# Tile 0's products with the first two value blocks between the late one-hot groups

## What is computed

```python
top_s, pos = lax.top_k(cand_s, PEER_TOPK)
experts = jnp.take_along_axis(cand_i, pos, axis=-1)
g = jax.nn.softmax(top_s, axis=-1)
a = jax.nn.gelu(jnp.einsum("td,thkd->thk", xc, u_tab[ec]))
out = jnp.einsum("thk,thkd->td", gc * a, v_tab[ec])
```

## Time and profile before

| | us |
|---|---|
| median of 3 runs | 2034.71 |
| lowest and highest | 2032.02, 2037.82 |
| span of the profiled execution | 2037.1 |
| TensorE busy | 1798.6 (88%) |
| VectorE busy | 1505.6 (74%) |
| ScalarE busy | 925.5 (45%) |
| GpSimd busy | 617.3 (30%) |

### The profile page before, as it was taken

One profiled execution on the slowest core, in us unless ns is written; L12 is line 12 of the kernel. 1 busy time (PEld: TensorE's weight loads), 2 busy tenths in 40 slices (PEclk: granted clock), 3 DMA queues, 4 the chain that ended last, 5 costly groups with the idle time before them and its releaser, 6 DMA issues.

```text
span 2037.1 us, 28687 instructions
## 1 busy us (share of the span) xinstructions
PE 1798.6 (88%) x11068; PEld 1601.8 (79%) x11068; DVE 1505.6 (74%) x1987; ACT 925.5 (45%) x1474; POOL 617.3 (30%) x549
## 2 busy tenths in 40 slices
PE   6999999999999999956875343699999999999997
PEld 5999999999999887756765243588888888888886
DVE  4464444444465548989889899977888889999997
ACT  5444444444443441123434899733344443433433
POOL 0000000001045003467777677112111114433430
PEclk9999999999999999978998556799999999999999
DMA  9565556556466869999999999498999999999994
GB/s 313 164 171 164 166 174 173 166 168 176 144 183 210 323 231 418 369 402 416 402 404 414 372 398 399 178 351 344 392 403 370 398 376 396 410 396 405 401 406 185
DMA packets 293543, 627.88 MB, mean 308 GB/s; under 512 B 10364, under 2 KB 223405, under 8 KB 234958
## 3 DMA queue, kind: packets, MB, share of 16 engines
q0 software_dynamic: 48400, 343.95, 42.0%
q1 hardware_dynamic: 244558, 282.20, 40.6%
q10 hardware_dynamic: 496, 0.58, 0.1%
HBM read 622.45 MB, written 8.44 MB: 310 GB/s over the span
## 4 chain that ended last, share of the span: by engine, by line
PE 71%; DVE 11%; issue 5%; ACT 4%; POOL 4%; DVEq 3%; DMA 2%; SPq 0%; POOLq 0%; ACTq 0%
PE ps L2019 35%; PE ps L1680 24%; DVE u_ring L1495 5%; PE ps L1861 4%; PE ps L1847 3%; DVEq L1445 3%; DMA u_ring<-in_peer_u,idx_all 2%; POOL u_ring L699 1%; POOL u_ring L708 1%; ACT ones L1132 1%; PE ps L1786 1%; PE ps L1767 1%; PE ps L1924 1%; PE ps L1984 1%; PE ps L1776 1%
## 5 line engine op out<-in xcount | busy, mean ns | idle before, releaser
L1254 DVE TENSOR_TENSOR w_lo<-raw,w_hi 128x2048 fp32r<-128x2048 f32 x112 | 259.1, 2313 | 322.7 <-ACT w_hi L781 322.7
L1680 PE MATMUL ps<-act_hi,w_hi 128*128 128x256 f32 x1536 | 442.2, 288 | 4.6 <-DVE act_lo L1378 2.9
L1680 PE MATMUL ps<-act_lo,w_hi 128*128 128x256 f32 x1536 | 435.8, 284 | 0.0
L1680 PE MATMUL ps<-act_hi,w_lo 128*128 128x256 f32 x1536 | 435.8, 284 | 0.0
L1189 ACT ACTIVATE v_hi<-v_raw 128x2048 fp32r<-128x2048 f32 x128 | 245.6, 1919 | 403.2 <-PE ps L2019 204.7
L2019 PE MATMUL ps<-v_hi,c_hi 128*128 128x512 f32 x1024 | 402.9, 393 | 1.2 <-DVE c_lo L1574 1.2
L2019 PE MATMUL ps<-v_hi,c_lo 128*128 128x512 f32 x1024 | 403.2, 394 | 0.0
L2019 PE MATMUL ps<-v_lo,c_hi 128*128 128x512 f32 x1024 | 402.1, 393 | 0.0
L1570 DVE TENSOR_TENSOR v_lo<-v_raw,v_hi 128x2048 fp32r<-128x2048 f32 x128 | 293.5, 2293 | 68.8 <-ACT v_hi L1189 68.3
L1495 DVE CUSTOM_DVE_ANT_0 u_ring<-u_ring,ps 128x2048 f32<-128x2048 f32 x144 | 326.3, 2277 | 19.9 <-DMA u_ring<-in_peer_u,idx_all 19.8
L781 ACT ACTIVATE w_hi<-raw 128x2048 fp32r<-128x2048 f32 x112 | 214.1, 1911 | 262.2 <-PE ps L1680 217.5
(11 more groups left out here) (246 smaller groups left out, 2267.6 us busy)
## 6 DMA issues: line engine op xcount, KB each, us to landing
v_raw<-in_peer_v SPq DMA_DIRECT2D x128, 1024.0 KB
raw<-in_w_in SPq DMA_DIRECT2D x80, 1024.0 KB
raw<-in_w_out SPq DMA_DIRECT2D x16, 1024.0 KB
wq<-in_peer_w_q SPq DMA_DIRECT2D x8, 2048.0 KB, 11.5
raw<-in_w_br_a SPq DMA_DIRECT2D x16, 512.0 KB
bias_by_query<-bias_by_distance POOLq DMA_DIRECT2D x1, 4096.0 KB, 20.6
bias_st<-bias_by_query POOLq DMA_DIRECT2D x16, 256.0 KB, 4.7
raw<-in_w_br_b SPq DMA_DIRECT2D x16, 256.0 KB
```

Source lines behind the costliest of these rows:

```text
L1254: nc.vector.tensor_tensor(w_lo[:, j % NHL], raw[:, j % NRAW], w_hi[:, j % NHL].bitcast(F32), ALU.subtract).then_inc(lo_done, 1)
L1680: last = nc.tensor.matmul(out_ap, w_parts[wp][:, slot, k], act_parts[ap][:, k], start=(k == k0 and m == 0), stop=(k == k1 - 1 and m == 2))
```

## The change

Tile 0's 24 products with value blocks 0 and 1 are put between the late groups: one behind each of the groups 2 to 12, then three, five and five. `TILE0_UPTO` gives how many are made before each group. The parts that they need are made earlier, by GpSimd: block 0's high part in two halves behind the gathers (10, 8) and (10, 10), its low part in four quarters behind (10, 13), (11, 1), (11, 3) and (11, 6); block 1's behind the last of GpSimd's own products of unit 11. ScalarE makes the high parts of tile 0's two matrices at (11, 11), GpSimd their low parts. Behind the groups, ScalarE and VectorE make tile 1's, and TensorE tile 1's 24 products of blocks 0 and 1. From block 2 on the loop is as it was. Loads and late operations take other places: block 1 is loaded once the last VectorE group is multiplied, block 2 after four late groups; the first row gather waits for late group 11, the second for block 0.

```diff
+TILE0_UPTO = [0, 0, 0] + list(range(1, 12)) + [14, 19, 24]
+FIRST_HIGH = [(10, 8), (10, 10)]
+FIRST_LOW = [(10, 13), (11, 1), (11, 3), (11, 6)]
...
-    b = n + n // 3 if n < 12 else n + 4 - max(n - LATE_OPS, 0) // 10
+    b = 1 if n == 0 else n + 2 + n // 4 if n < 12 else n + 4 - max(n - LATE_OPS, 0) // 10
...
         load_v(0)
-        sp.wait_ge(pk_pe, 2)
+        sp.wait_ge(dc_pe, DVE_GROUPS)
+        load_v(1)
+        sp.wait_ge(c_pe, ACT_GROUPS + 4)
         load_v(2)
-        sp.wait_ge(c_pe, ACT_GROUPS + 4)
-        load_v(1)
         sp.wait_ge(c_pe, ACT_GROUPS + LATE_GROUPS)
         load_v(3)
...
+        def first_high(b, dst, cols):
+            return nc.gpsimd.tensor_copy(dst[:, cols], v_raw[b][:, cols])
+        def first_low(b, hi, cols):
+            return nc.gpsimd.tensor_tensor(v_lo[b][:, cols], v_raw[b][:, cols], hi[:, cols].bitcast(F32), ALU.subtract)
...
             gather(u_ring[:, SLOT[n]], u_tab, u, k).then_inc(u_in[SLOT[n]], 16)
+            if (u, k) in FIRST_HIGH:
+                if k == FIRST_HIGH[0][1]:
+                    pool.wait_ge(v_in[0], 16)
+                    pool.wait_ge(sw_ok, NU - 1)
+                h = FIRST_HIGH.index((u, k))
+                first_high(0, v_hi0, slice(D // 2 * h, D // 2 * (h + 1))).then_inc(vh0_ok, 1)
+            if (u, k) in FIRST_LOW:
+                pool.wait_ge(vh0_ok, 2)
+                last = first_low(0, v_hi0, quarter(FIRST_LOW.index((u, k))))
...
+        pool.wait_ge(ch0_ok, 1)
+        for b in range(2):
+            nc.gpsimd.tensor_tensor(c_lo[b][:, 0], ct[:, 0, b], c_hi[0][:, b].bitcast(F32), ALU.subtract).then_inc(first_ok, 1)
+        pool.wait_ge(v_in[1], 16)
+        pool.wait_ge(dc_pe, DVE_GROUPS)
+        first_high(1, v_hi[hi_slot(1)], slice(0, D)).then_inc(vh0_ok, 1)
+        pool.wait_ge(vh0_ok, 3)
+        for c in range(4):
+            last = first_low(1, v_hi[hi_slot(1)], quarter(c))
+        last.then_inc(first_ok, 1)
...
             if n == 0:
                 pool.wait_ge(idx_ok, NU)
+                pool.wait_ge(c_pe, ACT_GROUPS + N_PRE)
             elif n == 1:
-                pool.wait_ge(c_pe, ACT_GROUPS + N_PRE)
+                pool.wait_ge(acc_ok, 1)
...
+            if (c, k) == (N_EARLY - 1, 4):
+                matrices(ACT_GROUPS - 1)
+            if (c, k) == (N_EARLY - 1, 11):
+                dve_group_out(DVE_GROUPS - 1)
+                first_keys(0)
...
-        high_v(0)
...
-        low_v(0)
-        dve.wait_ge(ch0_ok, 1)
-        low_c(0, 0, 1).then_inc(first_ok, 1)
+        dve.wait_ge(ch0_ok, 2)
+        for b in range(2):
+            nc.vector.tensor_tensor(c_lo[b][:, 1], ct[:, 1, b], c_hi[1][:, b].bitcast(F32), ALU.subtract).then_inc(vl_ok, 1)
...
         for g in range(LATE_GROUPS):
             late_matrices(g, g % 2)
+            for b, c, m in tile0_first[TILE0_UPTO[g]:TILE0_UPTO[g + 1]]:
+                if (c, m) == (0, 0):
+                    pe.wait_ge(first_ok, 4 if b else 2)
+                first_product(b, 0, c, m)
```

More of the change, by code:

```diff
@@ L316, in build @@
     pre = [at(f"pre{i}", kib, [P, 4, GTOK, PKEYS]) for i, kib in enumerate((192, 152, 128))]
-    early_dots = at("early_dots", 186, [P, N_EARLY, PTOP])
+    first_dots = at("first_dots", 186, [P, PH, PTOP])
+    early_dots = at("early_dots", 202.8125, [P, N_EARLY - PH, PTOP])
     late_dots = at("late_dots", 203.125, [P, 2, PTOP])
-    dots = [early_dots[:, u] if u < N_EARLY else late_dots[:, u % 2] for u in range(NU)]
+    dots = [first_dots[:, u] if u < PH else early_dots[:, u - PH] if u < N_EARLY else late_dots[:, u % 2] for u in range(NU)]
     gel = at("gel", 203.25, [P, 2, PTOP])
@@ L1072, in sum_of @@
             slot = u_ring[:, SLOT[PTOP * u + k]]
-            nc.scalar.activation(slot, slot, ACT.Copy, scale=0.5, accum_out=early_dots[:, u, k:k + 1]).then_inc(sum_dot, 1)
+            nc.scalar.activation(slot, slot, ACT.Copy, scale=0.5, accum_out=dots[u][:, k:k + 1]).then_inc(sum_dot, 1)
         def rows_turned(u, k):
@@ L1143, in one_hots, with first_keys @@
             last.then_inc(oh_ok, 1)
+        def first_keys(t):
+            act.wait_ge(c_ev, ACT_GROUPS + LATE_GROUPS * t)
+            act.wait_ge(dc_ev, DVE_GROUPS)
+            return nc.scalar.activation(c_hi[t][:, :], ct[:, t, 0:2], ACT.Copy).then_inc(ch0_ok, 1)
         for c, k in EARLY[2 * PTOP:]:
@@ L1207, in _ @@
             late_matrices(g)
-        act.wait_ge(c_ev, ACT_GROUPS + LATE_GROUPS)
-        for b in range(PKEYS):
-            t0 = 0 if b else 1
-            if b:
-                high_v(b)
-            nc.scalar.activation(c_hi[hi_slot(b)][:, t0:NT], ct[:, t0:NT, b], ACT.Copy).then_inc(ch_ok, 1)
-            for n in OPS_AT[b - 1] if b else ():
+        first_keys(1)
+        for b in range(2, PKEYS):
+            high_v(b)
+            if b == 2:
+                act.wait_ge(acc_ok, 1)
+            nc.scalar.activation(c_hi[hi_slot(b)][:, :], ct[:, :, b], ACT.Copy).then_inc(ch_ok, 1)
+            for n in OPS_AT[b - 1]:
                 if n < LATE_OPS and n % PTOP == PTOP - 1:
@@ L2020, in add_block @@
                                                     v_parts[vp][j % v_slots[vp]][:, WIDE * c:WIDE * c + WIDE],
-                                                    start=(first and j == 0 and m == 0), stop=(final and j == RING - 1 and m == 2))
+                                                    start=False, stop=(final and j == RING - 1 and m == 2))
                         if final and j == RING - 1 and c % 2:
```

60 lines of the change are left out of this document (34 added, 26 removed).

## The result

| | before | after |
|---|---|---|
| median, us (runs of both on one chip) | 2036.16 (10) | 2041.02 (10) |
| lowest and highest, us | 2032.02, 2040.76 (one run, at 2400.6, apart) | 2037.19, 2046.98 |
| ratio to before, 95% interval | | 1.0032 [1.0021, 1.0042] |
| span of the profiled execution, us | 2037.1 | 2035.9 |

The change made the kernel slower, by 4.9 us by the medians and 6.5 us by the ratio, whose interval is 4.3 to 8.6 us (before's median without the run apart is 2035.84). So the two spans can't be compared as they stand; what differs in favour of after lies ahead of the change.

A forecast was written before the change was run, and what follows sets the result against it. The value-block loop was taken as bound by TensorE alone, so work done earlier saves time. A 3.5 us gain, less 2.5 us of holds and 0.1 for block 2, gave -0.9 us: 2033.8 us from 2034.71, range 2029 to 2040.5.

The forecast's parts named there:

- The sum: Whole kernel: 3.5 us gained by the products, 2.5 lost to holds, 0.1 for block 2; net -0.9 us.
- A group is then 1.075 + 0.233 = 1.31 us of TensorE against a cycle of 1.215, so 0.09 us longer.: Late groups 2 to 11: one product each lengthens the cycle by 0.09 us, 0.9 us for the ten.
- each of the 19 products pushes the end by its whole 0.233 us: Late groups, rival: products add instead of filling, end 4.4 us later, not 1.5; 2036.6 us; chance 0.1.
- I take +2.5 us: Gather units 10 and 11: GpSimd's added pieces hold VectorE's operations for 2.5 us more.
- the proportional 3.6: Same holds: 7.2 us more GpSimd work, scaled by existing holds per product time, holds VectorE for 3.6 us.
- Just behind that train: cost 0: Block 1's GpSimd pieces, load taking 4.4 us, end at 1290.2, before VectorE's gelu step at 1290.4; no cost.
- worth nothing more: Work moved off ScalarE and VectorE, and the row gather issued after group 11: no gain beyond the sum.
- The rival on the slower side: GpSimd's longer trains hold VectorE through shared access, 7 us against 3.4 gained: +3.6, 2038.3 us; chance 0.27.
- with all bounds together: Whole kernel: the net effect reaches +6 us if all bounds coincide; no chance given.
- the start of tile 1's products: Behind the late groups: tile 1's first product comes 1.9 us after the last group.
- block 2 ready in time: Before block 2: its parts take 6.0 us behind ScalarE's moves, just hidden by 6.3 us on TensorE.
- the first late one-hot: Sign on VectorE: it would begin between 1291 and 1294 us in place of 1290.15.

The follow-up runs named there:

- e1: The kernel before, run again unchanged; no ratio given; 36.28 us from the turning of the picks to block 2's first product, late groups 21.31 us.
- e2: The changed kernel, run again unchanged; no ratio given; 35.96 us from the turning of the picks to block 2's first product, late groups 25.76 us.
- e5: The changed kernel with tile 0's products between late groups put mostly in twos; no ratio given; 34.49 us from the picks' turning to block 2's first product.
- e3: The changed kernel with all 24 products of tile 0 behind the last late group, none between groups; ratio to before 1.0030.
- e4: The changed kernel with GpSimd's pieces of block 0 moved from units 10 and 11 to behind its last product of unit 11; ratio to before 1.0018.
- e8: The changed kernel with block 0's pieces behind GpSimd's products, block 1's on ScalarE and VectorE, late dots later, no products between groups; no ratio; late groups 21.48 us.
- e11: e10 with all 24 products of tile 0 behind the last late group, none between groups; ratio to before 1.0014.
- e14: e12 with eight of block 0's products between late groups, in twos, and the other four behind the last group; ratio to before 0.9997.
- e10: The changed kernel with block 0's pieces behind GpSimd's products, block 1's on ScalarE (after picks' copies) and VectorE, block 0's twelve products paired between groups; ratio to before 1.0007.
- e12: e10 with GpSimd's block 0 pieces waiting for VectorE's last one-hot group, and late dots' first operations one block later, never two per block; ratio to before 1.0002.
- e13: The changed kernel with only the late dots' first operations moved one block later, never two in one block; ratio to before 1.0020.

## Why the prediction was wrong

The sum was -3.5 + 2.5 + 0.1 = -0.9 us; by the ratio it was +6.5. Three of its steps failed, and one thing was missing.

**"A group is then 1.075 + 0.233 = 1.31 us of TensorE against a cycle of 1.215, so 0.09 us longer."** A cycle was 1.52 us, 0.31 longer, since a single product between groups costs 0.43 us from its start to the next group's. I had taken the rate that products have behind each other; no row of before had a product next to a group but 1314.68, and that one (0.50 us long) I didn't use. The step fell by 0.2 us for each of ten cycles and for each of the later changes: the groups took 4.1 us longer (26.12 against 22.07; 4.5 between e1 and e2), not 1.5, and B gave 0.4 us at like clock in place of 3.5. As 0.233 us is what a product saves later, each one put there alone loses 0.08; a pair lengthens two cycles by 0.22 us (2.43 to 2.65) and saves 0.47, and so B is 0.6 shorter in e5 than with none between. The rival by which "each of the 19 products pushes the end by its whole 0.233 us" got 0.1 from me; e3 measures 0.25, so it was the one that came true; its reason, a longer loop through VectorE, did not (no idle time stands in the cycle).

**"I take +2.5 us"** for the holds. They were 4.8 and 5.2 us. The mechanism was the right one, and so were the prices of GpSimd's pieces: copies of 1.04 and 1.89 us (forecast 1.03 and 1.9), quarters of 1.28. What was undersized is the count of meetings. I walked the order with times of before and credited up to 2.3 us where the coefficients would miss their pair; they did in part (1.07 in place of 2.49), but everything later had moved as well, and a one-hot at 1236.64 and one at 1239.69 met a pair and a quarter instead. The 2.5 isn't the sum of the items that the walk names (+1.0, +0.6, up to -2.3); it is a choice below the proportional 3.6. That estimate was nearer: up to the last dot A took 3.4 us more, and it lacked only the step below. (It counts nine pairs of products, two of which hold nothing; from 1210 us to the last dot before has ten, four of which hold nothing, and the same rule then gives 3.2.) e4 shows the cause: without block 0's pieces in the units 2.1 us come back.

**"Just behind that train: cost 0"** for block 1. The term that was off is the load's: 4.4 us, read from how long the DMA engines were busy after an issue. It was issued at 1274.21 and GpSimd's copy could begin at 1281.22, 7.0 us later (7.1 in e2). So the train ended at 1288.1, the GELU step stood at 1286.05, and it and the coefficients were held 0.7 and 0.8 us. With 4.4 us the train would have ended ahead of the GELU. A margin of 0.2 us was no cover for that. Without this train on GpSimd the stretch from the last dot to the turning is 1.3 us again (e8 to e11, e14), where after has 2.8.

**Not in the prediction as a cost** were the rows of the late dots. I wrote that moving the row gather is "worth nothing more", which is right for what it gives, and didn't ask what its later place costs. Two buffers hold the rows of the first 14 late dots. A gather needs its dot's end, 0.94 to 2.83 us on GpSimd and up to 9.6 us to land; two blocks are 11.2 us, of which the dot itself takes 2.3. Before had issued both gathers ahead of block 0, the first at 1273.6 and the second at 1307.6. After issued its first at 1310.5 and the next two at 1322.5 and 1324.8, so that the dot beside block 3 waits for its row (to 1330.82), and its delay goes on to the gather that needs that dot's buffer, for block 5. In e10 that was the row 4.49 us late; a block more at the start (e12, e13) took the waits away.

The rival on the slower side named the cause, the access shared by GpSimd and VectorE, with +3.6 us. What made the result leave the 0.3% was that it came together with the rival of the added products; I had given chances to each alone. The prediction does name +6 "with all bounds together", but the range's upper end of 2040.5 us is about 2034.71 + 3.6 + 2 and leaves no room for it. The number missed the range by only 0.5 us, and part of that is the base: with ten runs before's median is 1.4 us higher than the 2034.71 that the forecast stood on. The Trainium skill (Advanced Engine Details and Errata, VectorE Performance Modes) says that VectorE's second SBUF port is shared with GpSimd and that the two block each other; the trace agrees, with VectorE rows stretched by 16.3 us beside GpSimd's.

**Right** were: the start of tile 1's products 1.96 us behind the last group (forecast 1.9), block 2 ready in time (no idle ahead of 1324.84; 5.7 us behind ScalarE's last move, forecast 6.0, though the four durations listed there add up to 6.9: the high part runs beside the dot), the value loop from there on unchanged (5.60 us per block; TensorE busy for 200 of 200 us from 1500), and that GpSimd's parts are there when TensorE wants them. Of the signs that I gave, those in absolute times could not decide anything: the first late one-hot (L1567) began at 1289.73, ahead of before's, in an execution that was 5.3 us ahead before A.

## What to carry to other kernels

Price work put into an engine's gaps by a row in which the two kinds of work stand side by side, and move it in blocks, not one at a time: here a single product per group lengthened the cycle by 0.31 us, and a pair per two groups by 0.22. Work given to an engine with room costs wherever it holds the engine that bounds the stage; keep such pieces out of that engine's exposed steps, and count new meetings over the whole shifted order, not only the old ones. When a prefetch gets a later place, check each of its next uses against issue, landing and the number of buffers, for its cost shows as scatter first (here 2037 to 2047 us) and in one profile hardly at all.

Before stages of two profiles are compared, the granted clock has to be compared: here it explains 0.8 us between two executions of one kernel, twice what the change gained in that stage.
